# Gate spreads as two fp32r products per token instead of one fp32 product

## The chip, the cores and the metric

The kernel runs on one core of one Trainium2 chip. The metric is the device time of one launch in microseconds (us), median of several runs.

## The reference

One decoder layer for 512 prompt tokens and 8 sample tokens (T = 520 rows, model width 2048). After attention, a state-space layer and an output projection comes a mixer of 128 x 128 = 16384 single-neuron experts, and this is the part concerned here:

```
s = einsum('thcd,hckd->thck', q, keys)            # 8 heads, 2 halves, 128 keys
s1, i1 = top_k(s[:, :, 0], 16);  s2, i2 = top_k(s[:, :, 1], 16)
top_s, top_p = top_k(s1[..., :, None] + s2[..., None, :], 16)
idx  = i1 * 128 + i2 at top_p                     # 8 x 16 = 128 experts per token
gate = softmax(top_s)
act  = gelu(einsum('thkd,td->thk', u_tab[idx], h))
out  = einsum('thk,thkd->td', gate * act, v_tab[idx])
```

A token thus has 128 choices, each with a first key, a second key and a gate. If the choices of a token are laid on the 128 partitions, the product of the one-hot rows of its second keys with the rows "one-hot of the first key times gate" is a 128 x 128 matrix: the token's gate for every expert.

## The kernel before, in words

The kernel is a sequence of stages: input projection, attention and state-space stages, output projection, stage e (expert keys, choices, and all experts' first product), stage f (all experts' second product). The first 128 rows (NA) take their 128 experts each by gathering rows of the expert table (GpSimd's indirect DMA, then a dot on VectorE, L1475). The other 392 rows (ND) go dense: all 128 groups of 128 experts (units) are multiplied, and the gates decide afterwards.

In stage e a dense unit is 48 products on TensorE (L1322 to L1324): 16 slices of the contraction, each three times, since both operands are split in a high and a low fp32r part. The unit's weights come by a DMA of SyncE (L102), ScalarE makes the high part (L107), GpSimd the low part (L111, a subtraction with both inputs in SBUF), and after each split GpSimd issues the next gather or two (L1198), for which it waits until a dot has freed one of four buffers.

For the gates of the dense rows, the 392 tokens are four tiles of 98 (DW). VectorE's `offer_choice(j)` (L1466) computes the softmax weights and looks up the two keys of every choice of tile j (`weigh`, `find_keys`, L1440 to L1464: casts, large two-input operations L1450 and L1452, reductions L1453) into the tile `gx`, at unit 11 + 8j. TensorE transposes them (`turn_choice`, L1332), ScalarE copies them to `gt` (L1266). Then, at units 16 + 8 x block + n with n from 0 to 6, VectorE makes the one-hot rows of four tokens (`one_hots`, L1478; it may be two batches ahead of TensorE; its input line of 0 to 127 lies in PSUM), TensorE multiplies them behind the dense products of the same unit (`spread`, L1335), and ScalarE copies the four 128 x 128 results from PSUM to `gs` (L1277). There are 14 blocks of 7 batches. VectorE's order in each unit is written out: due dots, then an offer if one is due, then the one-hots.

All queues are executed in order, with semaphores between the engines. `side_kept` counts ScalarE's copies of both kinds, `keys_ready` the one-hot batches, `spread_done` the spreads, `choice_turned` the transposed tiles.

Of the kernel before, what the change touches and what calls it, by code (L numbers as in the profile page):

```python
# [8 lines left out]
F32 = mybir.dt.float32  # L9
F32R = mybir.dt.float32r  # L10
I32 = mybir.dt.int32
U32 = mybir.dt.uint32
ALU = mybir.AluOpType
ACT = mybir.ActivationFunctionType
# [3 lines left out]
P = 128  # L18
# [1126 lines left out]
def stage_e(nc, m, ins, outs):  # L1145
# [6 lines left out]
    ug = [at(f"ug{j}", [P, D], F32, off=m.x0 + j * D * 4) for j in range(GW)]  # L1152
    hx = m.x0 + KT * T * 4
    gx = at("gx", [P, KT, T], F32, off=hx)
    keyrow = at("keyrow", [P, KT, T], F32, off=hx + KT * T * 4)
    m.top = m.free
    m.idx0 = at("idx0", [P, HK], I32); m.w0 = at("w0", [P, HK])
    m.kept = m.top
# [1 line left out]
    tpa = at("tpa", [P, HK], U32); sm = at("esm", [P, 1 + DT, 2, H])  # L1160
    idx = at("idx", [P, 1 + DT, H * 2, TK], U32); tv = at("tv", [P, 1 + DT, H, TK]); tp = at("tp", [P, 1 + DT, H, TK], U32)
    idf = at("idf", [P, H * 2, TK]); iota = at("iota", [P, P])
    ast = at("ast", [P, 2, ND]); gt = at("gt", [P, 3, ND]); eq = at("eq", [P, HK // 2, TK]); rs = at("rs2", [P, T])
    u0 = m.top
    stg = at("stg2", [P, 2, T]); htok = at("htok", [P, D]); keysT = at("keysT", [P, 16, P])
    m.top = u0
# [6 lines left out]
    with nc.Block() as block:  # L1173
# [28 lines left out]
        def _(act):  # L1202
# [40 lines left out]
            for e in range(N_EXP):  # L1243
                u, s = U_EXP_U + e, e % 2
                split_hi(m, act, u + 2, s, (u + 2) // 2, (m.mm_done, u + 3))
                if e >= 2:
                    act.wait_ge(st[s], 16 * (e // 2))
                act.activation(ast[:, s, :], m.acc[:, s, 0, 0:ND], ACT.Gelu_apprx_tanh).then_inc(m.acc_free, 1)
                act.wait_ge(m.acc_free, u + 3)
                act.dma_start(m.aD[e, :, :], ast[:, s, :]).then_inc(st[s], 16)  # L1250
                if e == 0:
                    keep_scores(H - 1)
                    act.wait_ge(S["scores_kept"], 2 * H)
                    act.wait_ge(S["tok_kept"], 4)
                    act.wait_ge(S["iota_in"], 16)
                    act.activation(m.acc[:, 1, 1, 0:P], iota[:, :], ACT.Copy).then_inc(S["iota_placed"], 1)
                    for g in range(4):
                        act.activation(m.aux[:, g, :], htok[:, 512 * g:512 * g + 512], ACT.Copy).then_inc(S["h_placed"], 1)
                if e == 9:
                    act.wait_ge(S["best_shifted"], 1 + DT)  # L1260
                    act.activation(tv[:, 0, :, :], tv[:, 0, :, :], ACT.Exp).then_inc(S["exps_ready"], 1)
                    act.activation(tv[0:DW, 1:1 + DT, :, :], tv[0:DW, 1:1 + DT, :, :], ACT.Exp).then_inc(S["exps_ready"], 1)
                if e in choice_of:
                    j = choice_of[e]
                    act.wait_ge(S["choice_turned"], j + 1)
                    act.activation(gt[:, :, DW * j:DW * j + DW], m.acc[:, 0, 1, 0:3 * DW].rearrange("p (x n) -> p x n", x=3), ACT.Copy).then_inc(S["side_kept"], 1)  # L1266
                    side += 1
                if e in batch_of:
                    b = batch_of[e]
                    blk, n = b // BB, b % BB  # L1270
                    act.wait_ge(S["spread_done"], b + 1)
                    if n == 0:
                        if blk >= 2:
                            act.wait_ge(S["gates_stored"], 16 * (blk - 1))
                        if blk == 0:
                            act.wait_ge(S["h_placed"], 4)
                    act.activation(gs[blk % 2][:, :, 4 * n:4 * n + 4].rearrange("p e t -> p t e"), m.acc[:, 0, 1, :].rearrange("p (t e) -> p t e", t=4), ACT.Copy).then_inc(S["side_kept"], 1)  # L1277
                    side += 1
                    if n == BB - 1:
                        act.wait_ge(S["side_kept"], side)  # L1280
                        act.dma_start(m.gD[blk, :, :, :].rearrange("p e n -> p (e n)"), gs[blk % 2][:, :, :].rearrange("p e n -> p (e n)")).then_inc(S["gates_stored"], 16)
# [7 lines left out]
        def _(pe):  # L1289
# [37 lines left out]
            def turn_choice(j, ready, side):  # L1327
                pe.wait_ge(S["choice_ready"], ready)
                if side is not None:
                    pe.wait_ge(S["side_kept"], side)  # L1330
                for x in range(3):
                    mm = pe.transpose(m.acc[:, 0, 1, DW * x:DW * x + DW], gx[0:DW, j * 3 + x, 0:P], m.ident[0:DW, 0:DW])  # L1332
                mm.then_inc(S["choice_turned"], 1)

            def spread(n, b, side):  # L1335
                pe.wait_ge(S["keys_ready"], b + 1)
                pe.wait_ge(S["side_kept"], side)
                for t in range(4):
                    r = 4 * (n % 2) + t
                    mm = pe.matmul(m.acc[:, 0, 1, P * t:P * t + P], keyrow[:, r, 0:P], keyrow[:, 8 + r, 0:P], start=True, stop=True)  # L1340
                mm.then_inc(S["spread_done"], 1)

            first_query()
# [30 lines left out]
        def _(dve):  # L1374
# [10 lines left out]
            def ch(ins):  # L1385
                after(done(ins))
# [51 lines left out]
            def find_keys(t, out):  # L1438
                n = ROWS[t]
                ch(dve.tensor_copy(idf[0:n, :, :], idx[0:n, t, :, :]))  # L1440
                il = idf[0:n, :, :].rearrange("p (h c) k -> p h c k", c=2)
                for c in range(2):
                    if c == 0:
                        ch(dve.tensor_scalar(tpa[0:n, :], tp[0:n, t, :, :].rearrange("p h k -> p (h k)"), 4, None, ALU.logical_shift_right))
                    else:
                        ch(dve.tensor_scalar(tpa[0:n, :], tp[0:n, t, :, :].rearrange("p h k -> p (h k)"), 15, None, ALU.bitwise_and))
                    ch(dve.tensor_copy(pf[0:n, :], tpa[0:n, :]))
                    for g in range(2):
                        half = slice(HK // 2 * g, HK // 2 * (g + 1))
                        ch(dve.tensor_tensor(eq[0:n, :, :], pf[0:n, half].unsqueeze(2).broadcast_to([n, HK // 2, TK]), iota[0:n, 0:TK].unsqueeze(1).broadcast_to([n, HK // 2, TK]), ALU.is_equal))  # L1450
                        e4 = eq[0:n, :, :].rearrange("p (h k) j -> p h k j", h=H // 2)
                        ch(dve.tensor_tensor(e4, e4, il[:, 4 * g:4 * g + 4, c, :].unsqueeze(2).broadcast_to([n, H // 2, TK, TK]), ALU.mult))  # L1452
                        ch(dve.tensor_reduce(out(c)[:, half], eq[0:n, :, :], AX.X, ALU.add))  # L1453
# [6 lines left out]
            def weigh(t, out):  # L1460
                n = ROWS[t]
                ch(dve.tensor_reduce(sm[0:n, t, 0, :], tv[0:n, t, :, :], AX.X, ALU.add))
                ch(dve.reciprocal(sm[0:n, t, 1, :], sm[0:n, t, 0, :]))
                ch(dve.tensor_tensor(out.rearrange("p (h k) -> p h k", h=H), tv[0:n, t, :, :], sm[0:n, t, 1, :].unsqueeze(2).broadcast_to([n, H, TK]), ALU.mult))  # L1464

            def offer_choice(j):  # L1466
                weigh(1 + j, gx[0:DW, 3 * j, 0:P])
                find_keys(1 + j, lambda c: gx[0:DW, 3 * j + 1 + c, 0:P])
                dve.sem_inc(S["choice_ready"], 1)

            def dot(k):
# [6 lines left out]
            def one_hots(b):  # L1478
                n = b % BB
                if b == 0:  # L1480
                    dve.wait_ge(S["iota_placed"], 1)
                if n == 0 and b > 0:
                    dve.wait_ge(S["spread_done"], b)
                elif b >= 2:
                    dve.wait_ge(S["spread_done"], b - 1)
                line = m.acc[:, 1, 1, 0:P]
                for t in range(4):
                    c, r = 4 * b + t, 4 * (n % 2) + t
                    dve.tensor_scalar(keyrow[:, r, 0:P], line, gt[:, 2, c:c + 1], None, ALU.is_equal)
                    x = dve.tensor_scalar(keyrow[:, 8 + r, 0:P], line, gt[:, 1, c:c + 1], gt[:, 0, c:c + 1], ALU.is_equal, ALU.mult)  # L1490
                x.then_inc(S["keys_ready"], 1)

            for h in range(H):
# [8 lines left out]
            for e in range(N_EXP):  # L1502
                if e == 9:
                    dve.wait_ge(S["exps_ready"], 2)
                    weigh(0, g0[:, :])
                while k < dots_by(e):
                    dot(k)
                    k += 1
                if e + 4 in choice_of:
                    offer_choice(choice_of[e + 4])  # L1510
                if e in batch_of:
                    b = batch_of[e]
                    if (4 * b + 3) // DW != (4 * b - 1) // DW:
                        j = (4 * b + 3) // DW
                        dve.wait_ge(S["side_kept"], 8 * j + 1)
                    one_hots(b)
            while k < HK:
                dot(k)
# [316 lines left out]
```

## Time and profile before

| | |
|---|---|
| Median of 3 runs | 4014.96 us (4014.14 to 4015.8) |
| Profiled execution, its own time | 4018.7 us |
| Its span, first to last instruction | 4016.9 us |
| TensorE matmuls busy | 3763.5 us (94%) |
| TensorE weight loads busy | 3442.9 us (86%) |
| VectorE busy | 2039.2 us (51%) |
| GpSimd busy | 2064.2 us (51%) |
| ScalarE busy | 1078.1 us (27%) |
| Mean granted TensorE clock | 0.951 of 2.4 GHz |

Engines are named PE (TensorE matmul), PEld (TensorE weight load), DVE (VectorE), ACT (ScalarE), POOL (GpSimd), SP (SyncE). L1340 is line 1340 of the kernel. Matmuls overlap each other and their weight loads, so the busy share of PE doesn't tell the pace; the distance between two starts does. The whole span counts every stage; the change touches only the stretch from about 1754 to 2821 us.

### The profile page before, as it was taken

What the parts mean: (1) busy time and instruction counts of PE and PEld (TensorE: products, weight loads), DVE (VectorE), ACT (ScalarE), POOL (GpSimd) and SP (SyncE); (2) the same over time, 40 slices, a digit from 0 to 9 for tenths busy, and PEclk for the clock granted to TensorE, in tenths of its full rate; (3) what the DMA queues carried; (4) which work ended last, traced back from release to release, by engine and by line L of the source; (5) the groups of instructions that cost most, each with busy time, mean ns of one, the idle gap of its engine ahead of it and who ended that gap; (6) DMA issues with size and microseconds to landing.
All of it is one profiled execution on the core that took longest, in us unless ns stands there. A gap on an engine that the chain in (4) does not pass through costs nothing. (4 is left out here: it accounts for less than half of the span.)

```text
span 4016.9 us, 60164 instructions
## 1 busy us (share of the span) xinstructions
PE 3763.5 (94%) x22816; PEld 3442.9 (86%) x22816; DVE 2039.2 (51%) x3661; ACT 1078.1 (27%) x1146; POOL 2064.2 (51%) x985
## 2 busy tenths in 40 slices
PE   8999689998879899999999999999799999999997
PEld 8988543336679899999999999999799999999997
DVE  4221343320330159786644454454477677777773
ACT  3111132211142222323333333333222222222222
POOL 3333267400043444565566556665466766777672
PEclk9999889995589899999999999999899999999999
DMA  5578646554232212366777777776777777877773
GB/s 215 205 286 308 166 157 217 191 170 40 53 138 105 103 64 84 146 250 237 266 277 273 283 278 268 296 279 258 294 291 294 285 290 296 300 297 289 290 291 111
DMA packets 293750, 897.84 MB, mean 224 GB/s; under 512 B 120993, under 2 KB 154274, under 8 KB 216610
## 3 DMA queue, kind: packets, MB, share of 16 engines
q1 hardware_dynamic: 226114, 557.11, 40.7%
q0 software_dynamic: 36864, 268.45, 16.4%
q10 hardware_dynamic: 30624, 70.46, 4.8%
q8 instruction: 73, 1.20, 0.1%
q14 instruction: 75, 0.61, 0.0%
HBM read 822.74 MB, written 70.84 MB: 222 GB/s over the span
## 5 line engine op out<-in xcount | busy, mean ns | idle before, releaser
L111 POOL TENSOR_TENSOR wl<-raw,wh 128x2048 fp32r<-128x2048 f32 x324 | 1528.4, 4717 | 1423.6 <-ACT wh L107 1423.5
L107 ACT ACTIVATE wh<-raw 128x2048 fp32r<-128x2048 f32 x324 | 620.4, 1915 | 2080.4 <-PE acc L1324 726.2
L1653 PE MATMUL acc<-vh,wh 128*128 128x392 f32 x2048 | 704.2, 344 | 43.1 <-DVE xt L1718 21.9
L1322 PE MATMUL acc<-hh,wh 128*128 128x392 f32 x2048 | 710.4, 347 | 1.4 <-POOL wl L111 1.4
L1323 PE MATMUL acc<-hl,wh 128*128 128x392 f32 x2048 | 698.7, 341 | 0.0
L1654 PE MATMUL acc<-vl,wh 128*128 128x392 f32 x2048 | 696.6, 340 | 0.0
L1324 PE MATMUL acc<-hh,wl 128*128 128x392 f32 x2048 | 696.4, 340 | 0.0
L1655 PE MATMUL acc<-vh,wl 128*128 128x392 f32 x2048 | 695.6, 340 | 0.0
L126 PE MATMUL acc<-hh,wh 128*128 128x264 f32 x1984 | 567.1, 286 | 11.7 <-issue 10.9
L127 PE MATMUL acc<-hl,wh 128*128 128x264 f32 x1984 | 561.5, 283 | 0.0
L128 PE MATMUL acc<-hh,wl 128*128 128x264 f32 x1984 | 560.0, 282 | 0.0
L1475 DVE SCALAR_TENSOR_TENSOR ug<-ug,aux 128x2048 f32<-128x2048 f32 x128 | 292.4, 2287 | 315.7 <-DMA ug<-expert_u,idx 315.5
L1653 PEld LDWEIGHTS acc<-vh,wh 128*128 128x128 f32 x2048 | 385.2, 188 | 54.9 <-DVE xt L1718 32.7
L126 PEld LDWEIGHTS acc<-hh,wh 128*128 128x128 f32 x1984 | 374.9, 189 | 31.9 <-issue 30.4
L1718 DVE TENSOR_TENSOR xt<-xt,acc 128x392 f32<-128x392 f32 x512 | 273.5, 557 | 234.4 <-PE acc L1655 228.1
L1322 PEld LDWEIGHTS acc<-hh,wh 128*128 128x128 f32 x2048 | 385.7, 188 | 1.8 <-issue 1.8
L1323 PEld LDWEIGHTS acc<-hl,wh 128*128 128x128 f32 x2048 | 385.8, 188 | 0.0
L1324 PEld LDWEIGHTS acc<-hh,wl 128*128 128x128 f32 x2048 | 385.4, 188 | 0.0
L1654 PEld LDWEIGHTS acc<-vl,wh 128*128 128x128 f32 x2048 | 385.3, 188 | 0.1
L1655 PEld LDWEIGHTS acc<-vh,wl 128*128 128x128 f32 x2048 | 385.2, 188 | 0.0
L127 PEld LDWEIGHTS acc<-hl,wh 128*128 128x128 f32 x1984 | 374.7, 189 | 0.4
L128 PEld LDWEIGHTS acc<-hh,wl 128*128 128x128 f32 x1984 | 374.6, 189 | 0.0
(288 smaller groups left out, 4230.7 us busy)
## 6 DMA issues: line engine op xcount, KB each, us to landing
raw<-units SPq DMA_DIRECT2D x324, 1024.0 KB, 4.8
kr<-cache_k SPq DMA_DIRECT2D x128, 512.0 KB, 6.0
vr<-cache_v SPq DMA_DIRECT2D x256, 256.0 KB, 3.1
expert_acts<-ast ACTq DMA_DIRECT2D x128, 196.0 KB, 3.0
expert_gates<-gs ACTq DMA_DIRECT2D x14, 1792.0 KB, 6.5
a<-expert_acts SPq DMA_DIRECT2D x32, 784.0 KB, 8.9
g<-expert_gates SPq DMA_DIRECT2D x32, 784.0 KB, 11.2
xt<-x_t SPq DMA_DIRECT2D x4, 1040.0 KB, 10.0
```

Source lines behind the costliest of these rows:

```text
L107: act.activation(m.wh[s][:, :, :], m.raw[s][:, :, :], ACT.Copy).then_inc(m.hi_done, 1)
L111: pool.tensor_tensor(m.wl[s][:, :, :], m.raw[s][:, :, :], m.wh[s][:, :, :].bitcast(F32), ALU.subtract).then_inc(m.lo_done, 1)
L126: pe.matmul(o, m.wh[s][:, k, :], rhs_hi[:, k, c0:c0 + n], start=(k == k_range[0]), stop=False)
L127: pe.matmul(o, m.wh[s][:, k, :], rhs_lo[:, k, c0:c0 + n], start=False, stop=False)
L128: mm = pe.matmul(o, m.wl[s][:, k, :], rhs_hi[:, k, c0:c0 + n], start=False, stop=(k == k_range[-1]))
L1322: pe.matmul(o, m.wh[s][:, k, :], m.hh[:, k, NA:T], start=(k == 0), stop=False)
L1323: pe.matmul(o, m.wh[s][:, k, :], m.hl[:, k, NA:T], start=False, stop=False)
L1324: mm = pe.matmul(o, m.wl[s][:, k, :], m.hh[:, k, NA:T], start=False, stop=(k == KT - 1))
L1475: dve.scalar_tensor_tensor(ug[k % GW][:, :], ug[k % GW][:, :], 1.0, m.aux[:, :, :].rearrange("p a n -> p (a n)"), ALU.mult, ALU.mult, accu ...
L1653: pe.matmul(o, m.wh[s][:, 4 * e + d, :], vh[gg][:, e, :], start=(e == 0), stop=False)
L1654: pe.matmul(o, m.wh[s][:, 4 * e + d, :], vl[gg][:, e, :], start=False, stop=False)
L1655: mm = pe.matmul(o, m.wl[s][:, 4 * e + d, :], vh[gg][:, e, :], start=False, stop=(e == GRP - 1))
```

## The change

The gate row is split in two fp32r parts: `gth`, the gate row rounded to fp32r by a second copy of ScalarE from PSUM, and the rest, `gt` minus `gth`, which VectorE computes in place once for each tile of 98 tokens. For each token VectorE now makes three one-hot rows instead of two: second key, first key times rounded gate, first key times rest. TensorE multiplies the first with each of the other two, all fp32r, accumulating in PSUM. To make room, `gx` keeps two tiles of choices instead of four (so an offer from the third on waits for an earlier transposition), and `lowrow` lies behind it.

```
-    keyrow = at("keyrow", [P, KT, T], F32, off=hx + KT * T * 4)
+    keyrow = at("keyrow", [P, KT, T], F32R, off=hx + KT * T * 4)
+    lowrow = at("lowrow", [P, KT - 6, T], F32R, off=hx + 6 * T * 4)
...
+    gth = at("gth", [P, ND], F32R)                     # added beside gt
...
-                    act.activation(gt[...], m.acc[:, 0, 1, 0:3 * DW]..., ACT.Copy).then_inc(S["side_kept"], 1)
+                    act.activation(gt[...], m.acc[:, 0, 1, 0:3 * DW]..., ACT.Copy)
+                    act.activation(gth[:, DW * j:DW * j + DW], m.acc[:, 0, 1, 0:DW], ACT.Copy).then_inc(S["side_kept"], 1)
...
-                    mm = pe.transpose(..., gx[0:DW, j * 3 + x, 0:P], m.ident[0:DW, 0:DW])
+                    mm = pe.transpose(..., gx[0:DW, j % 2 * 3 + x, 0:P], m.ident[0:DW, 0:DW])
...
-                    mm = pe.matmul(m.acc[:, 0, 1, P * t:P * t + P], keyrow[:, r, 0:P], keyrow[:, 8 + r, 0:P], start=True, stop=True)
+                    pe.matmul(m.acc[:, 0, 1, P * t:P * t + P], keyrow[:, r, 0:P], keyrow[:, 8 + r, 0:P], start=True, stop=False)
+                    mm = pe.matmul(m.acc[:, 0, 1, P * t:P * t + P], keyrow[:, r, 0:P], lowrow[:, r, 0:P], start=False, stop=True)
...
             def offer_choice(j):
+                if j >= 2:
+                    dve.wait_ge(S["choice_turned"], j - 1)
-                weigh(1 + j, gx[0:DW, 3 * j, 0:P])
-                find_keys(1 + j, lambda c: gx[0:DW, 3 * j + 1 + c, 0:P])
+                weigh(1 + j, gx[0:DW, j % 2 * 3, 0:P])
+                find_keys(1 + j, lambda c: gx[0:DW, j % 2 * 3 + 1 + c, 0:P])
...
-                    x = dve.tensor_scalar(keyrow[:, 8 + r, 0:P], line, gt[:, 1, c:c + 1], gt[:, 0, c:c + 1], ALU.is_equal, ALU.mult)
+                    dve.tensor_scalar(keyrow[:, 8 + r, 0:P], line, gt[:, 1, c:c + 1], gth[:, c:c + 1].bitcast(F32), ALU.is_equal, ALU.mult)
+                    x = dve.tensor_scalar(lowrow[:, r, 0:P], line, gt[:, 1, c:c + 1], gt[:, 0, c:c + 1], ALU.is_equal, ALU.mult)
...
                         dve.wait_ge(S["side_kept"], 8 * j + 1)
+                        low = gt[:, 0, DW * j:DW * j + DW]
+                        ch(dve.tensor_tensor(low, low, gth[:, DW * j:DW * j + DW].bitcast(F32), ALU.subtract))
                     one_hots(b)
```

`ch` makes VectorE wait for the instruction's completion before the next.

## Rows read from the trace of the kernel before

**Rows 1.** Busy time by stretch: us and records (x) of each engine, granted clock.

```profile
1760.00:1900.00 140.00, 126.86 (x725) 126.16 (x724) 114.08 (x176) 44.61 (x39) 79.55 (x28) 0.95 0.62 235
...
2300.00:2500.00 200.00, 200.00 (x1175) 200.00 (x1174) 100.39 (x200) 69.78 (x60) 122.33 (x46) 1.00 0.72 280
```

**Rows 2.** What TensorE waited for, whole span: us in total, times, longest.

```profile
PE acc L1340 <- DVE keyrow L1490: 19.5, 3, 6.8
```

**Rows 3.** Timeline of TensorE, spreads: start us, us, line, operands, records.

```profile
1762.90 1.05 PE L1340 MATMUL acc<-keyrow 128*128 128x128 f32 x8
1772.38 1.05 PE L1340 MATMUL acc<-keyrow 128*128 128x128 f32 x8
```

**Rows 4.** Timeline of TensorE, fp32r products of 264 and of 392 columns.

```profile
1454.83 0.28 PE L127 MATMUL acc<-hl,wh 128*128 128x264 f32 x1
...
1455.80 0.29 PE L126 MATMUL acc<-hh,wh 128*128 128x264 f32 x1
...
1801.81 0.34 PE L1322 MATMUL acc<-hh,wh 128*128 128x392 f32 x1
...
1808.96 0.34 PE L1323 MATMUL acc<-hl,wh 128*128 128x392 f32 x1
```

**Rows 5.** Weight loads grouped by line and shape, whole span: busy us, mean ns.

```profile
L1323 PEld LDWEIGHTS acc<-hl,wh 128*128 128x128 f32 x2048 | 385.8, 188 | 0.0
...
L753 PEld LDWEIGHTS aux<-vr,wb 128*8 128x8 f32 x512 | 43.9, 92 | 178.8 <-issue 175.0 <-DMA vr<-cache_v 0.9
...
L1313 PEld LDWEIGHTS aux<-keysT,stg 128*98 128x98 f32 x128 | 14.9, 165 | 0.0
```

**Rows 6.** Timeline, 128 weight columns and one moved column, matmuls and loads.

```profile
908.14 1.05 PE L741 MATMUL aux<-ident,pvs 8*128 8x1 f32 x8
...
908.14 0.96 PEld L741 LDWEIGHTS aux<-ident,pvs 8*128 8x128 f32 x8
```

**Rows 7.** Timeline of VectorE at the first batch of one-hots.

```profile
1757.45 0.35 DVE L1489 TENSOR_SCALAR keyrow<-acc,gt 128x128 f32<-128x128 f32 x1 [9.26 <-ACT gt L1266]
1757.72 0.40 DVE L1490 TENSOR_SCALAR keyrow<-acc,gt 128x128 f32<-128x128 f32 x1
1758.04 0.34 DVE L1489 TENSOR_SCALAR keyrow<-acc,gt 128x128 f32<-128x128 f32 x1
```

**Rows 8.** Timeline of GpSimd, splits ahead of the first stall and, last, the second.

```profile
1756.28 4.62 POOL L111 TENSOR_TENSOR wl<-raw,wh 128x2048 fp32r<-128x2048 f32 x1 [4.20 <-ACT wh L107]
...
1774.63 5.05 POOL L111 TENSOR_TENSOR wl<-raw,wh 128x2048 fp32r<-128x2048 f32 x1 [3.76 <-ACT wh L107]
...
1784.09 5.46 POOL L111 TENSOR_TENSOR wl<-raw,wh 128x2048 fp32r<-128x2048 f32 x1 [2.50 <-ACT wh L107]
...
1793.57 5.21 POOL L111 TENSOR_TENSOR wl<-raw,wh 128x2048 fp32r<-128x2048 f32 x1 [2.11 <-ACT wh L107]
...
1877.28 4.76 POOL L111 TENSOR_TENSOR wl<-raw,wh 128x2048 fp32r<-128x2048 f32 x1 [2.55 <-ACT wh L107]
```

**Rows 9.** Timeline of VectorE, offer before the first stall.

```profile
1771.00 0.28 DVE L1462 TENSOR_REDUCE esm<-tv 98x8 f32<-98x128 f32 x1
...
1785.10 5.53 DVE L1452 TENSOR_TENSOR eq<-eq,idf 98x1024 f32<-98x1024 f32 x1
...
1793.18 1.23 DVE L1452 TENSOR_TENSOR eq<-eq,idf 98x1024 f32<-98x1024 f32 x1
...
1795.82 0.35 DVE L1489 TENSOR_SCALAR keyrow<-acc,gt 128x128 f32<-128x128 f32 x1 [0.16 <-DVE gx L1453]
```

**Rows 10.** Timeline of TensorE, the spread behind the first stall.

```profile
1798.28 2.08 PE L1340 MATMUL acc<-keyrow 128*128 128x128 f32 x8 [6.79 <-DVE keyrow L1490]
```

**Rows 11.** Timeline of VectorE, dot before and end of the offer ahead of the second stall.

```profile
1852.02 2.29 DVE L1475 SCALAR_TENSOR_TENSOR ug<-ug,aux 128x2048 f32<-128x2048 f32 x1 [1.93 <-DMA ug<-expert_u,idx]
...
1876.46 1.22 DVE L1452 TENSOR_TENSOR eq<-eq,idf 98x1024 f32<-98x1024 f32 x1
```

**Rows 12.** Timeline of VectorE, a dot in a normal unit.

```profile
2450.26 2.29 DVE L1475 SCALAR_TENSOR_TENSOR ug<-ug,aux 128x2048 f32<-128x2048 f32 x1 [1.38 <-DMA ug<-expert_u,idx]
```

More of the change, by code:

```diff
@@ L1162, in stage_e @@
     idf = at("idf", [P, H * 2, TK]); iota = at("iota", [P, P])
-    ast = at("ast", [P, 2, ND]); gt = at("gt", [P, 3, ND]); eq = at("eq", [P, HK // 2, TK]); rs = at("rs2", [P, T])
+    ast = at("ast", [P, 2, ND]); gt = at("gt", [P, 3, ND]); gth = at("gth", [P, ND], F32R); eq = at("eq", [P, HK // 2, TK]); rs = at("rs2", [P, T])
     u0 = m.top
@@ L1265, in _ @@
                     act.wait_ge(S["choice_turned"], j + 1)
-                    act.activation(gt[:, :, DW * j:DW * j + DW], m.acc[:, 0, 1, 0:3 * DW].rearrange("p (x n) -> p x n", x=3), ACT.Copy).then_inc(S["side_kept"], 1)
+                    act.activation(gt[:, :, DW * j:DW * j + DW], m.acc[:, 0, 1, 0:3 * DW].rearrange("p (x n) -> p x n", x=3), ACT.Copy)
+                    act.activation(gth[:, DW * j:DW * j + DW], m.acc[:, 0, 1, 0:DW], ACT.Copy).then_inc(S["side_kept"], 1)
                     side += 1
@@ L1331, in turn_choice @@
                 for x in range(3):
-                    mm = pe.transpose(m.acc[:, 0, 1, DW * x:DW * x + DW], gx[0:DW, j * 3 + x, 0:P], m.ident[0:DW, 0:DW])
+                    mm = pe.transpose(m.acc[:, 0, 1, DW * x:DW * x + DW], gx[0:DW, j % 2 * 3 + x, 0:P], m.ident[0:DW, 0:DW])
                 mm.then_inc(S["choice_turned"], 1)
```

## The prediction

> **What bounds the kernel now.** I read the busy time by stretch first. While the spreads run, TensorE is busy 200.00 of 200 us at full clock in most stretches, but only 126.86 of 140 us between 1760 and 1900 us [rows 1]. So in this stage the end is set by TensorE's own instructions, plus a few holes. The list of what TensorE waited for names the holes: three waits of a spread (L1340) for one-hot rows from VectorE (L1490), 19.5 us in all, the longest 6.8 us [rows 2]. The timeline of TensorE gives the price of a spread: it begins at 1762.90 and again at 1772.38, a period of 9.48 us [rows 3]. A dense unit has 48 products; 40 of them take 1808.96 - 1801.81 = 7.15 us, 178.8 ns each, so 48 take 8.58 us [rows 4]. A spread therefore costs 9.48 - 8.58 = 0.89 us, and there are 98 of them (14 blocks of 7), 87 us in all. It shows as 8 records, two for each fp32 product: 0.89 / 8 = 111 ns a record. That is what the change works on.
>
> **The change on TensorE.** Four fp32 products (8 records) become eight fp32r products. The dense products, fp32r too, are one record each, so I expect 8 records again; what matters is their pitch at 128 moved columns. The streamed part: fp32r products of 264 columns start every (1455.80 - 1454.83) / 8 = 121.2 ns, those of 392 columns every 178.8 ns [rows 4]. That is 0.450 ns a column and 2.4 ns fixed, so 128 columns would stream in 60 ns. The load part: a weight load lasts 92 ns for 8 columns, 165 ns for 98 and 188 ns for 128 columns [rows 5], a slope of 0.80 ns a column, so loading 128 columns occupies some 102 ns; the 188 ns row is an fp32r load, so this form is not loaded faster. Whether that bounds the pitch is seen where the moved part is almost nothing: eight records with 128 weight columns and one moved column take 0.96 us of loads, 186 ns the single one, so (0.96 - 0.19) / 7 = 110 ns apart; the matmuls give (1.05 - 0.25) / 7 = 114 ns [rows 6]. So a load of 128 columns can't come more often than every 110 ns. Each of the eight new products brings its own load, as each dense product does [rows 4, 5]. I take 111 ns, so the spread still costs 0.89 us: **gain 0 us**. Bounds: 60 ns gives 98 x 8 x 51 = 40 us faster; the 264-column row, 121 ns, gives 98 x 8 x 10 = 8 us slower. The nearest rows are those of rows 6 and the spreads' own 111 ns, because they have the same 128 weight columns.
>
> Here the Trainium skill speaks for the change. "TensorE: Matmul & The Clock Gate" (Back-to-back issue gap) gives a stream of load and matmul pairs about 81 ns each at N=128. By it a spread would be 0.65 us and the sum some 22 us better than mine. The rows with 128 weight columns stand at 110 ns and the measurement decides.
>
> **The change on VectorE: normal units.** Each token gets a third one-hot. The first instruction of a token takes a step of 1757.72 - 1757.45 = 0.27 us and the second 1758.04 - 1757.72 = 0.32 us [rows 7]; the new one has the form of the second. A batch of four grows from 2.32 to 3.58 us, by 1.27 us; 98 batches are 124 us more on VectorE, whose idle time takes most of it. In a normal unit the one-hots are followed by a dot, which waited 1.38 us for its gathered row [rows 12], more than 1.27 us, and the keys are made more than a unit early. Cost 0. If that cover were gone, a dot would come late, and GpSimd, which waits for it before a gather, would hold back the next weight split; I see no such wait of TensorE now.
>
> **The first spread.** VectorE now starts at 1757.45, when the gates arrive from ScalarE [rows 7]. New ahead of the one-hots are ScalarE's extra copy and a subtraction with both inputs in SBUF. GpSimd's split runs from 1756.28 for 4.62 us, to 1760.90 [rows 8]. What happens to a VectorE operation with two SBUF inputs inside a split is seen in the offer: L1452 at 1785.10 took 5.53 us, to 1790.63, where the split from 1784.09 took 5.46 us, to 1789.55; the same line at 1793.18 took 1.23 us [rows 8, 9]. So it waits for the split's end and then runs. The one-hots read PSUM and aren't held (0.35 us within a split, [rows 7, 8]). The subtraction thus ends near 1761.2 whatever the extra copy costs, and the one-hots at 1764.8 instead of 1759.8. TensorE wants them at 1762.7: a new hole of 2.1 us.
>
> **The three stalls.** Before the first, VectorE has no idle time from 1757.45 on: one-hots, dot, one-hots, dot, one-hots, dot, then the offer at 1771.00 [rows 9]. With 2.2 us a dot (2.29 in [rows 12], its end beside the next start) the offer now begins at 1761.2 + 3 x 3.58 + 3 x 2.21 = 1778.6, 7.6 us later. GpSimd's splits move by the 2.1 us of the first hole: to 1776.8, 1786.2 and 1795.7, from 1774.63, 1784.09 and 1793.57 [rows 8]. Today the offer meets two splits and its last two-input operation begins at 1793.18, 0.4 us ahead of the third [rows 9]. Moved by 7.6 us it meets the third too. Stepped through with 1.26 us for each large operation: the small two-input one waits until 1781.8, a large one from 1786.7 until 1791.8, another from 1795.8 until 1801.0; the rest ends at 1808.8 and the one-hots of batch 3 at 1812.5. They ended at 1798.1 before, where TensorE resumed (1798.28, after 6.79 us [rows 10]). So everything behind is **14.4 us later**, the first hole included. TensorE restarts at the lower clock (1.2 GHz) in either kernel: those eight records took 2.08 us instead of 1.05 [rows 3, 10]. Without the third split the delay is 5.7 us.
>
> For stalls two and three the dot before the offer waited for its gathered row (1.93 us ahead of stall two [rows 11]), so a longer batch of one-hots (1.27 us) fits in, and the offer starts when it did. Only the one-hots behind the offer are longer: 2 x 1.27 = **2.5 us**. Risk: in the offer before stall two the last two-input operation starts at 1876.46 and the split at 1877.28 [rows 8, 11]; a slip of 0.8 us adds a wait of some 4.6 us there, and likewise before stall three. The new wait for choice_turned is for transposes done twelve units earlier: 0. The remaining subtractions have more than a unit of slack: 0. The two gx changes only move addresses.
>
> **Sum.** The profiled execution took 4018.7 us with a span of 4016.9. 4018.7 + 0 + 14.4 + 2.5 = 4035.6 us. The median of the runs is 4015.0, 3.7 below the profiled one, so I forecast **4032 us** (own range 4024 to 4040). A measurement of this kernel can tell about 0.2%, 8 us, from no change.
>
> **Rivals.**
> - *Loads hide entirely* (faster). If short fp32r products go at their streamed 60 ns, each spread costs 0.48 us. Seven spreads ahead of stalls gain nothing, since the keys decide there; 91 x 0.41 = 37 us, less 16.9, is 20 us faster, 3995; if the offers' slips then meet their splits, 4004. I say 4000. It decides from a pitch under about 77 ns on, where 91 x 8 x 34 ns = 25 us are the 16.9 us and 8 more. For it: dense products hide their loads under the streams. Against it: [rows 6]. The same page of the Trainium skill (Weight-path perf modes) says the fast weight load is on for 128 weights if the type is not FP32; were fp32r taken so, this rival holds. The 188 ns of an fp32r load against 165 ns for 98 columns speaks against it [rows 5].
> - *Loads hide in part.* Halfway, 85 ns: 91 x 8 x 26 ns = 19 us gained, 16.9 lost: 4013, within noise. The page's 81 ns belongs here.
> - *The third split is missed*, because the subtraction or the offer falls otherwise: 5.7 + 2.5 = 8 us, 4023.
> - *The offers before stalls two and three slip into their third split*: 4.6 us each more, 4041.
> - *A short fp32r product isn't single-pass* but runs as two fp32 records, 221 ns: a spread costs 1.77 us, 98 x 0.89 = 87 us more, with the stalls some 4119. For it nothing in the trace, which has no fp32r product under 256 columns; so it can't be excluded.
>
> **Chances.** Forecast 0.50, loads hide entirely 0.14, in part 0.12, third split missed 0.10, slips 0.09, not single-pass 0.05. Faster: 0.14 and a third of the partial case, 0.18. Within 0.2%: the rest of that and half of the missed split, 0.14. Slower 0.68. The range 4000 to 4045 leaves out the lower half of the first rival, the last rival and little else.
>
> **What would show it.** TensorE: eight records a spread 110 ns apart, spread period still 9.48 us (right); 9.0 us or less, or 10 and more (wrong). VectorE: 3.58 us a batch, L1490's new neighbour 0.40 us; a subtraction of 3 us or more at the first spread. Waits: L1340 for VectorE four times instead of three, some 36 us instead of 19.5, the longest near 19 us. If the waits hardly grow, or TensorE's spread period shrinks, my prediction is wrong.

## The result, and the profile after

The changed kernel takes 4030.6 us (median of 7 runs, 4028.73 to 4033.71) against 4014.96 us before (7 runs, 4014.07 to 4018.61). The ratio is 1.0038, with a 95% interval of 1.0026 to 1.0050: slower by 10 to 20 us. I forecast 4032 us. The profiled execution of after took 4030.41 us, with a span of 4028.6.

First the spreads on TensorE, after, as [rows 3] show them for before. The first row of the first spread, rows of the second (start us, us), and the first rows of the third and the fourth:

```profile
1763.42 0.33 PE L1342 MATMUL acc<-keyrow 128*128 128x128 f32 x1 [1.73 <-DVE lowrow L1496]
...
1772.99 0.22 PE L1342 MATMUL acc<-keyrow 128*128 128x128 f32 x1
1773.05 0.28 PE L1343 MATMUL acc<-lowrow,keyrow 128*128 128x128 f32 x1
1773.16 0.27 PE L1342 MATMUL acc<-keyrow 128*128 128x128 f32 x1
...
1773.73 0.27 PE L1343 MATMUL acc<-lowrow,keyrow 128*128 128x128 f32 x1
...
1782.46 0.22 PE L1342 MATMUL acc<-keyrow 128*128 128x128 f32 x1
...
1809.06 0.47 PE L1342 MATMUL acc<-keyrow 128*128 128x128 f32 x1 [16.98 <-DVE lowrow L1496]
```

Two things are to be seen. Eight products again, the inner ones (1773.73 - 1773.05) / 6 = 113 ns apart, and a period of 1782.46 - 1772.99 = 9.47 us where it was 9.48: TensorE gained nothing. And two holes, 1.73 us at the first spread, where there was none, and 16.98 us at the fourth, where there were 6.79 [rows 10]. Over the whole span the list of TensorE's waits says (us, times, longest):

```profile
PE acc L1342 <- DVE lowrow L1496: 34.4, 4, 17.0
```

against 19.5 us in 3 [rows 2]: 14.9 us more. The four are 1.73, 16.98, 7.95 and 7.69 us. The rows of the last two:

```profile
1894.51 0.48 PE L1342 MATMUL acc<-keyrow 128*128 128x128 f32 x1 [7.95 <-DVE lowrow L1496]
...
1979.69 0.48 PE L1342 MATMUL acc<-keyrow 128*128 128x128 f32 x1 [7.69 <-DVE lowrow L1496]
```

The stretches (columns as in [rows 1]) tell the same: TensorE is busy 13.5 us less in the stretch that holds the first hole and the first two stalls, and fully busy in a later one, as before.

```profile
1760.00:1900.00 140.00, 113.34 (x643) 112.32 (x642) 123.34 (x210) 41.26 (x37) 73.48 (x26) 0.90 0.62 232
...
2300.00:2500.00 200.00, 200.00 (x1179) 200.00 (x1178) 121.18 (x272) 72.55 (x63) 120.29 (x45) 1.00 0.74 288
```

The medians count every stage of the kernel; the traces can count the changed stretch alone. It begins with the first transposition of a tile of choices and ends with the last copy of gates (durations in ns, then first and last start in us). Before:

```profile
L1332 PE MATMUL acc<-ident,gx x12: 245/247/249, 1754.0 to 2005.3; 98*128 98x98 f32 x12
...
L1277 ACT ACTIVATE gs<-acc x98: 1166/1197/1220, 1765.9 to 2822.9; 128x512 f32<-128x512 f32 x98
```

After:

```profile
L1334 PE MATMUL acc<-ident,gx x12: 245/247/249, 1752.7 to 2020.0; 98*128 98x98 f32 x12
...
L1279 ACT ACTIVATE gs<-acc x98: 1167/1194/1230, 1764.6 to 2836.7; 128x512 f32<-128x512 f32 x98
```

That is 1068.9 us before and 1084.0 after, 15.1 us more, so the loss of 15.6 us between the medians arises in this stretch. Of each pair the first line gives the start and the second the end. Below, "the stretch" of a kernel is this time.

Now VectorE from the first batch to the fourth (this place comes 1.35 us earlier than in the trace of before: the split of 1756.28 [rows 8] starts at 1754.93; so add 1.35 when comparing with [rows 7 to 9]):

```profile
1756.24 3.41 DVE L1523 TENSOR_TENSOR gt<-gt,gth 128x98 f32<-128x98 f32 x1 [9.42 <-ACT gth L1268]
1759.68 0.35 DVE L1494 TENSOR_SCALAR keyrow<-acc,gt 128x128 fp32r<-128x128 f32 x1
1759.95 0.40 DVE L1495 TENSOR_SCALAR keyrow<-acc,gt,gth 128x128 fp32r<-128x128 f32 x1
1760.27 0.40 DVE L1496 TENSOR_SCALAR lowrow<-acc,gt 128x128 fp32r<-128x128 f32 x1
...
1777.07 0.28 DVE L1465 TENSOR_REDUCE esm<-tv 98x8 f32<-98x128 f32 x1
...
1777.63 2.41 DVE L1467 TENSOR_TENSOR gx<-tv,esm 98x128 f32<-98x128 f32 x1
...
1784.83 5.59 DVE L1453 TENSOR_TENSOR eq<-pf,iota 98x1024 f32<-98x1024 f32 x1
...
1794.75 5.40 DVE L1455 TENSOR_TENSOR eq<-eq,idf 98x1024 f32<-98x1024 f32 x1
...
1805.33 0.35 DVE L1494 TENSOR_SCALAR keyrow<-acc,gt 128x128 fp32r<-128x128 f32 x1 [0.16 <-DVE gx L1456]
...
1808.60 0.40 DVE L1496 TENSOR_SCALAR lowrow<-acc,gt 128x128 fp32r<-128x128 f32 x1
```

and GpSimd's splits in the same stretch:

```profile
1754.93 4.60 POOL L111 TENSOR_TENSOR wl<-raw,wh 128x2048 fp32r<-128x2048 f32 x1 [4.22 <-ACT wh L107]
...
1775.25 4.63 POOL L111 TENSOR_TENSOR wl<-raw,wh 128x2048 fp32r<-128x2048 f32 x1 [5.75 <-ACT wh L107]
...
1784.72 4.62 POOL L111 TENSOR_TENSOR wl<-raw,wh 128x2048 fp32r<-128x2048 f32 x1 [3.73 <-ACT wh L107]
...
1794.17 4.90 POOL L111 TENSOR_TENSOR wl<-raw,wh 128x2048 fp32r<-128x2048 f32 x1 [2.93 <-ACT wh L107]
```

Read them side by side. The subtraction (L1523) of 98 columns takes 3.41 us and ends at 1759.65, just behind the split's end at 1759.53; its other three took 0.26 us. The offer (L1465) begins at 1777.07. It meets three splits: L1467 ends behind the first, L1453 at 1790.42 behind the second (end 1789.34), L1455 at 1800.15 behind the third (1799.07). The one-hots of batch 3 end at 1809.0.

Where the added 124 us of one-hots went is seen in VectorE's own waits, for gathered rows (in us, times, longest), before and after:

```profile
DVE ug L1475 <- DMA ug<-expert_u,idx: 315.5, 107, 10.1
```

```profile
DVE ug L1480 <- DMA ug<-expert_u,idx: 205.0, 85, 8.6
```

VectorE waited 110.5 us less for gathered rows. The third one-hots took the place of waits.

### The profile page after: what moved, and what is told of

It reads as the page before. It is cut to its first block and busy times, and to the rows that moved or that the text cites. A ratio compares the mean times of both kernels' runs of the same rounds, so it can differ in the third digit from the quotient of the medians.

```text
span 4028.6 us, 60564 instructions
## 1 busy us (share of the span) xinstructions
PE 3750.5 (93%) x22816; PEld 3433.3 (85%) x22816; DVE 2162.2 (54%) x4057; ACT 1079.6 (27%) x1150; POOL 2060.3 (51%) x985
```

## The experiments

Times are medians; the kernel before ran beside each group (4015.4, 4015.8 and 4015.4 us). Some of these kernels leave part of the work out, and the text says which.

**Only TensorE's part.** The second product takes the rounded gate row again; ScalarE's extra copy stays.

```
-                    dve.tensor_scalar(keyrow[:, 8 + r, 0:P], ...)
-                    x = dve.tensor_scalar(lowrow[:, r, 0:P], ...)
+                    x = dve.tensor_scalar(keyrow[:, 8 + r, 0:P], ...)
...
-                    mm = pe.matmul(..., keyrow[:, r, 0:P], lowrow[:, r, 0:P], start=False, stop=True)
+                    mm = pe.matmul(..., keyrow[:, r, 0:P], keyrow[:, 8 + r, 0:P], start=False, stop=True)
...
-                        ch(dve.tensor_tensor(low, low, gth[...].bitcast(F32), ALU.subtract))
```

> The changed kernel without the third one-hot row and without the subtraction: the second product of each token takes the rounded-gate row again, so the gates are wrong (twice the rounded gate) but TensorE runs the same eight fp32r products a spread, and VectorE's batch is back at 2.32 us. Theory (the loss is VectorE's, TensorE gains nothing): waits of the spreads for VectorE near 19.5 us in three again, spread period 9.47 us, 4015 to 4018 us. Rival 1 (fp32r products cost TensorE time somewhere, or the clock falls): stays near 4030. Rival 2 (TensorE did gain and VectorE hid it): clearly under 4015, by up to 40 us, with a spread period under 9.3 us.

Measured 4020.2 us (11 runs, 4016.29 to 4023.27), ratio to before 1.0010 (1.0000 to 1.0019). The waits are those of before:

```profile
PE acc L1342 <- DVE keyrow L1495: 19.8, 3, 7.0
```

So TensorE's part neither gains nor brings the loss. The median is 5 us above that of before, 2 above what I expected, and up to 8 us are left in the interval; the profiled execution had a span of 4016.4 us, 0.5 below that of before. In the traces the stretch takes 1070.9 us, 2.0 more than before, and the restarts behind the three stalls account for it. The first stall ends at 1798.28 in both traces; the 6.3 us behind it (columns as in [rows 1], granted clock third from the end) in before and in this kernel:

```profile
1798.30:1804.60 6.30, 6.30 (x30) 6.30 (x31) 6.30 (x11) 1.17 (x1) 1.43 (x2) 0.75 0.72 273
```

```profile
1798.30:1804.60 6.30, 6.30 (x22) 6.30 (x23) 6.30 (x11) 1.18 (x1) 1.43 (x2) 0.51 0.71 274
```

Behind its three stalls TensorE was back at full clock after 6.4, 7.0 and 3.8 us, in before after 3.2, 5.4 and 3.1. Behind the first stall of before, the eight records and four dense products took 3.17 us, and 1.60 at full clock elsewhere in the stretch. Summed up in this way the restarts cost 8.1 us here and 5.6 in before, though the stalls are as long. So a restart has no fixed price, and it differs between executions. The other 3 of the 5 us lie outside the stretch or in the noise; no run shows a cause for them.

**Only VectorE's part**, with the fp32 products of before.

```
-    keyrow = at("keyrow", [P, KT, T], F32R, ...)
+    keyrow = at("keyrow", [P, KT, T], F32, ...)
...
-                    pe.matmul(..., keyrow[:, r, 0:P], keyrow[:, 8 + r, 0:P], start=True, stop=False)
-                    mm = pe.matmul(..., keyrow[:, r, 0:P], lowrow[:, r, 0:P], start=False, stop=True)
+                    mm = pe.matmul(..., keyrow[:, r, 0:P], keyrow[:, 8 + r, 0:P], start=True, stop=True)
```

> The changed kernel with the fp32 products of before: the third one-hot row, the extra copy and the subtraction are all made, but the low row is not multiplied and the product takes the rounded gate row, so the rest of the gate is left out. Theory: VectorE's part alone brings the whole loss, 4028 to 4033 us, waits of the spreads about 34 us in four, with a longest of 17. Rival 1 (TensorE's products cost the time): near 4015 to 4018. Rival 2 (TensorE gained something that VectorE's loss hides): slower than 4033.

Measured 4031.4 us (4028.99 to 4033.38), ratio 1.0038 (1.0024 to 1.0051), the same as the whole change:

```profile
PE acc L1342 <- DVE lowrow L1495: 34.3, 4, 17.0
```

Its stretch takes 1085.0 us against 1084.0 of the whole change. The loss is VectorE's, and swapping the products is worth nothing that can be told from noise.

**The offers cut in four**, in the changed kernel and in the kernel before. Part q looks up one key (q // 2) for one half of the choices (q % 2); part 0 also computes the softmax weights.

```
-                if e + 4 in choice_of:
-                    offer_choice(choice_of[e + 4])
+                for q in range(4):
+                    if e + 4 - q in choice_of:
+                        offer_part(choice_of[e + 4 - q], q)
```

> The changed kernel, with each offer of choices cut in four parts of some 6 us, done in four successive units instead of one of 25 us. Theory: no stall of 17 or 8 us is left, at most the one of 1.7 us at the first spread; 32.6 us of waits and three restarts at the lower clock (1.6 us each) go: 3991 to 3997 us. Rival 2 (part of the loss comes from VectorE's load in normal units, through late dots, gathers and splits): stalls go, but 5 us or more above the same cut of the kernel before.

> The kernel before with the same cut of the offers. Theory: 19.5 us of waits and three restarts (4.8 us) go: 3989 to 3993 us, so the change on top of the cut costs 1 to 4 us (the first spread's hole), not 15. Rival 2: the change still costs 8 us or more. If the stalls aren't the loss at all: near 4015.

Measured 3990.97 us (3990.47 to 3995.86; ratio 0.9943, 0.9929 to 0.9956) and 3990.07 us (3984.68 to 3993.41; ratio 0.9935, 0.9921 to 0.9948). In the cut changed kernel one wait of the spreads is left, in the other none is listed:

```profile
PE acc L1342 <- DVE lowrow L1512: 1.7, 1, 1.7
```

The change costs 0.9 us between the medians on this base, instead of 15.6. The two intervals are each some 11 us wide, so the medians alone leave several us open; the stretches are 1045.7 and 1043.4 us, 2.3 apart, of which 1.7 are the one wait that is left. So nearly the whole loss is longer stalls, and the third one-hot in 98 units hides where VectorE has idle time. Both are faster than either kernel of this case, by 24 and 25 us against before.

**What sets the pitch**, on the base of the cut changed kernel. Half of the weight columns; half of the moved columns; bf16 in place of fp32r; one product instead of two:

```
64 weight columns:  pe.matmul(m.acc[0:64, 0, 1, ...], keyrow[:, r, 0:64], keyrow[:, 8 + r, 0:P], ...)   # and the low row likewise
64 moved columns:   pe.matmul(m.acc[:, 0, 1, P * t:P * t + 64], keyrow[:, r, 0:P], keyrow[:, 8 + r, 0:64], ...)
bf16:               keyrow, lowrow in BF16; gate rounded to bf16 by ScalarE; low = gate - rounded gate
one product:        mm = pe.matmul(..., keyrow[:, r, 0:P], keyrow[:, 8 + r, 0:P], start=True, stop=True), no low row
```

These are the edits in short. The kernels with 64 columns also fill the PSUM rows once, so that the copies read something defined; the one with one product also makes no low row and no subtraction on VectorE.

> The changed kernel with the cut offers (4 parts), and the spreads' eight fp32r products with only 64 of the 128 weight columns: the gates of experts 64 to 127 of each second-key half are left out. Theory (the load of the weights sets the pitch): pitch falls to the streamed 60 ns, a spread to about 0.5 us, and with no stalls left the time by up to 98 x 8 x 51 ns = 40 us: about 3951 us. Rival (a fixed price of a short fp32r product, or two passes over the moved columns, 107 ns): pitch stays at 110 ns and the time at 3991.

> The same base, with all 128 weight columns but only 64 of the 128 moved ones, so half of the gates is left out again. Theory: pitch stays at 110 ns, 3991 us. Rival (two passes over the moved columns): pitch falls to 55 to 60 ns, about 3951.

> The changed kernel with cut offers and with one-hot rows and gates in bf16: the gate in two bf16 parts instead of two fp32r parts. The Trainium skill (TensorE: Matmul & The Clock Gate, Weight-path perf modes) has a faster weight load for 128 weights of a type that is not FP32. In rows: if it is so, the load row falls well under 188 ns and the pitch to between 55 and 81 ns, 98 x 8 x (30 to 55 ns) = 24 to 43 us less than 3991: 3948 to 3967. Rival (loads of 128 columns cost 107 ns in every type): 3991.

> Cut offers and only the product with the rounded gate, four fp32r products a spread; the rest of the gate is left out. Theory: 111 ns each for the four products taken away, 98 x 4 x 0.111 = 43.5 us, so 3990 - 43 = 3947 us, with VectorE's batch at 2.32 us. Rival (a lone fp32r product costs more than one of a pair that share their weights): spread over 0.6 us, 3960 or more.

Measured, in this order: 3958.1 us (3955.57 to 3962.43), 3993.2 (3993.14 to 3995.57), 3957.7 (3957.1 to 3959.81), 3944.8 (3939.46 to 3949.85). The weight loads while the spreads run (behind the bar: busy us, mean ns of one) with 64 weight columns:

```profile
L1343 PEld LDWEIGHTS acc<-keyrow 128*64 128x64 f32 x392 | 49.9, 135 | 2.0 <-DVE lowrow L1513 2.0
```

with 64 moved columns:

```profile
L1343 PEld LDWEIGHTS acc<-keyrow 128*128 128x128 f32 x392 | 74.8, 191 | 2.0 <-DVE lowrow L1513 2.0
```

and in bf16:

```profile
L1343 PEld LDWEIGHTS acc<-keyrow 128*128 128x128 bf16 x392 | 35.8, 97 | 18.1 <-issue 16.0 <-DVE lowrow L1513 2.0
```

The starts of successive products of one spread, with 64 weight columns, 60 ns apart:

```profile
2294.01 0.22 PE L1343 MATMUL acc<-keyrow 128*64 128x128 f32 x1
2294.07 0.22 PE L1344 MATMUL acc<-lowrow,keyrow 128*64 128x128 f32 x1
...
2294.43 0.22 PE L1344 MATMUL acc<-lowrow,keyrow 128*64 128x128 f32 x1
```

with 64 moved columns, 112 ns apart:

```profile
2296.95 0.28 PE L1344 MATMUL acc<-lowrow,keyrow 128*128 128x64 f32 x1
...
2297.62 0.28 PE L1344 MATMUL acc<-lowrow,keyrow 128*128 128x64 f32 x1
```

and in bf16, 57 ns apart:

```profile
2296.48 0.23 PE L1343 MATMUL acc<-keyrow 128*128 128x128 bf16 x1
...
2296.88 0.22 PE L1344 MATMUL acc<-lowrow,keyrow 128*128 128x128 bf16 x1
```

Halving what streams changes nothing (the stretch is 1046.5 us against 1045.7), halving what is loaded brings the pitch to the 60 ns that the stream needs: the load is the bound, shown from both sides. The gain is 32.9 us where I expected 40. I had let all eight intervals shrink, from a spread's first product to the dense product behind it. The first of them is 60 ns in the changed kernel too (1772.99 to 1773.05 above), so seven shrink (the last of them from 0.11 to 0.06 us): 98 x 7 x 51 ns = 35 us. The stretch is 35.9 us shorter. In bf16 the load takes half the time, and the kernel gains 33.3 us, its stretch 36.8. One product instead of two, with the rest of the gate left out, gains 46 us, 3 more than the 43.5 expected; without the third one-hots and the subtraction the hole of 1.7 us is gone too.

**The stall's inside.** The subtraction taken out; and the third one-hot taken out for the first three batches alone, with the first subtraction:

```
-                        ch(dve.tensor_tensor(low, low, gth[...].bitcast(F32), ALU.subtract))        # first kernel
...
+                        if j > 0:                                                                   # second kernel
...
-                    x = dve.tensor_scalar(lowrow[:, r, 0:P], ...)
+                    if b >= 3:
+                        x = dve.tensor_scalar(lowrow[:, r, 0:P], ...)
```

> The changed kernel without the subtraction: the low row carries the whole gate, so the product counts it twice. Theory (a GpSimd split holds VectorE's operations with two SBUF inputs to its end): the hole of 1.7 us at the first spread goes and the first offer starts some 3.2 us earlier, but within it the third split still holds a large operation, so that it ends less than 1 us earlier, and the time is within 1 us of the changed kernel's 4030.6. Rival (the offer's length doesn't depend on the splits): it ends 3.2 us earlier, 4027.

> The changed kernel with only two one-hot rows for the first three batches (their products take the rounded gate twice) and without the subtraction for the first tile: only what lies ahead of the first offer is as before, everything behind it as in the changed kernel. Theory: the offer starts when it did before and misses the third split again; the first stall is 6.8 + 1.3 = 8 us instead of 17, no hole at the first spread, sum of waits about 23.5 us, and of the 15.6 us of loss some 11 go: 4018 to 4021. Rival (the later 95 batches with three rows cost the time): at least 4026.

Without the subtraction: 4032.2 us (4027.27 to 4036.9), ratio to before 1.0042 (1.0028 to 1.0056), waits:

```profile
PE acc L1342 <- DVE lowrow L1496: 32.5, 3, 17.0
```

The hole at the first spread is gone, and the time is where the changed kernel's was, within noise. Counted from the moment at which the gates are ready, the offer starts 3.4 us earlier (17.4 us against 20.8) and the one-hots behind it 2.0 us earlier (47.1 against 49.1). I had expected less than 1, the rival 3.2. The trace decides for the theory and shows what I had missed: with the hole gone TensorE, and the splits with it, run earlier too. The held operation and the third split in this kernel:

```profile
1795.50 5.40 DVE L1455 TENSOR_TENSOR eq<-eq,idf 98x1024 f32<-98x1024 f32 x1
```

```profile
1794.93 4.89 POOL L111 TENSOR_TENSOR wl<-raw,wh 128x2048 fp32r<-128x2048 f32 x1 [2.93 <-ACT wh L107]
```

The split ends 40.8 us behind the gates, and 42.8 in the changed kernel: 2.0 us earlier, as the one-hots are. From the split's end to the one-hots are 6.3 us in both. So here the end of the third split sets the end of the offer, and not the offer's start. The 1.9 us of waits that went were taken back by the restarts, 8.3 us in this trace against 6.7 in that of the changed kernel.

Two rows for the first three batches: 4020.6 us (11 runs, 4016.6 to 4026.62), ratio 1.0015 (1.0006 to 1.0024), as expected. The waits:

```profile
PE acc L1342 <- DVE lowrow L1498: 23.6, 3, 8.2
```

The last two-input operation of its offer, and the third split:

```profile
1789.86 1.22 DVE L1456 TENSOR_TENSOR eq<-eq,idf 98x1024 f32<-98x1024 f32 x1
```

```profile
1790.09 5.36 POOL L111 TENSOR_TENSOR wl<-raw,wh 128x2048 fp32r<-128x2048 f32 x1 [1.95 <-ACT wh L107]
```

The operation gets in 0.23 us ahead of the split, as in before (0.4 us), and nothing of this offer waits for the third split. Three batches of 98, and one small subtraction, made 10.0 of the 15.6 us between the medians (10.8 us of waits, and 10.4 of the stretch, which is 1073.6 us). The intervals of the two ratios leave some 6 us either way.

## Why the prediction was right

**TensorE, gain 0.** Right. The period is 9.47 us for 9.48, the inner pitch 113 ns for a forecast 111, and the two half-width kernels show the reason that [rows 5, 6] gave: 128 columns of fp32 or fp32r weights are never loaded more often than every 110 ns in the rows of these traces. ([rows 6] may be compared with the spreads: the granted clock is 1.00 there, from 905 to 910 us.) The rival with hidden loads and the one with half-hidden loads fall, and so does the one of a short fp32r product in several passes. The 81 ns of the Trainium skill ("TensorE: Matmul & The Clock Gate", Back-to-back issue gap) isn't reached with fp32r; with bf16 the same products go at 57 ns. Its rule of a faster load for 128 weights of a type that is not FP32 (Weight-path perf modes) agrees for bf16, 97 ns a load against 191; fp32r loads like fp32. My bound for the rival with hidden loads was too large by one interval in eight, as told above.

**VectorE in normal units, cost 0.** Right: after the three stalls no spread waits, the waits for gathered rows shrank by 110.5 us, and on the cut base the stretch is 2.3 us longer, 1.7 of it the first spread's hole.

**The first spread, a hole of 2.1 us.** Right in mechanism, 1.73 us measured. The subtraction did wait for the split's end. The Trainium skill says that a VectorE instruction with two SBUF inputs contends with a GpSimd one that reads SBUF ("SBUF — State Buffer", Who interferes with whom); the trace agrees, 3.41 us instead of 0.26.

**Stall one, 14.4 us later.** The mechanism was right: the offer began at 1777.07, with the 1.35 us of offset 1778.4 where I had 1778.6, and it met the third split. The size was 2.1 us too large. The one-hots ended at 1809.0 + 1.35 = 1810.4, not 1812.5. I had let the first two splits last 5.05 and 5.46 us as in [rows 8]; those had themselves been held up by VectorE. The one of 1784.09 began inside this operation of the kernel before:

```profile
1783.84 1.23 DVE L1450 TENSOR_TENSOR eq<-pf,iota 98x1024 f32<-98x1024 f32 x1
```

The two splits now lasted 4.63 and 4.62, the large operation behind the second was through about 1 us earlier, and one more large operation fit in ahead of the third split: that one held L1455, where I had it hold the L1453 ahead of it. That is 1.26 of the 2.1 us. On TensorE's own waits the term is 1.73 + 16.98 - 6.79 = 11.9 us.

**Stalls two and three, 2.5 us.** 7.95 and 7.69 against 6.34 and 6.36 before: 2.9 us. Neither slipped into its third split, but the first of them came near: its last two-input operation began 0.50 us ahead of the split (0.82 before), that of the other 0.76. In their case the dots' gather waits took up the longer batch, as forecast: the dot before the offer still waited 1.04 and 0.37 us, from 1.93 and 1.72.

**The sum.** 14.4 + 2.5 = 16.9 us forecast, 11.9 + 2.9 = 14.9 us more of waits in the traces (rounded at each step), 15.6 us between the medians. Right. That the forecast of 4032 lies within 1.4 us of the median is in part luck: stall one was too large by 2 us, and the interval of the measured loss is 10 us wide. One thing was taken as equal, the restart at the lower clock: the three cost 5.6 us in the trace of before and 6.7 in that of after, worked out as above, though the stalls were 6.3 to 6.8 us there and 7.7 to 17.0 here. The price of the rival in which the third split is missed, 5.7 us, has no working behind it: taking the third wait, 1795.8 to 1801.0, out of the 14.4 us leaves 9.2. No run shows that case. Of the 5 us of the kernel with TensorE's part alone, 2.0 are longer restarts in its one trace; what the rest is, if it is anything, stays open.

## What to carry to other kernels

In fp32 and fp32r a product with 128 weight columns and 128 or fewer moved columns was bound by its weight load (111 to 113 ns); a type with fewer passes a product doesn't help if each pass brings its own load. Count loads, not passes, and for exact operands such as one-hots try the type that loads faster. Before adding work to an engine that looks half idle, find the one long block in its order for which others wait: here cutting that block in four was worth 25 us in the kernel before and 40 in the changed one, and the added work then cost 1 to 2 us. And when work ahead of a block moves, look at which operations of the other engine it now meets (here GpSimd's third split).

## What I had not expected of the hardware

- A bf16 load of 128 columns lasts 97 ns against 191 for fp32r, and the products follow every 57 ns instead of 111 to 113: 33 us for the 98 x 7 = 686 intervals. The changed kernel with cut offers and two bf16 parts of the gate takes 3957.7 us, 0.9854 of before (0.9838 to 0.9871); with the rounded fp32r gate alone, the rest left out, 3944.8 us, 0.9818 (0.9802 to 0.9835).
- GpSimd's split is held up by VectorE as well as the other way round: 4.6 us when VectorE is quiet, 5.46 us in an offer of the kernel before, where it began inside a VectorE operation with two SBUF inputs. Such a duration belongs to its neighbours and can't be carried over to another phase.
- What a restart costs doesn't follow the length of the stall. Behind 16.98 us of idle time TensorE ran at 1.2 GHz (granted clock 0.50) for 4.7 us; behind stalls of 6.3 to 7.0 us it did so for 3.1 to 7.0 us. In before that cost 1.5 to 2.5 us a stall, in the kernel with TensorE's part alone up to 3.2.
